# Column units beside layer 0's attention, logits ahead of the last value unit, and constant products in TensorE's waits

## What is computed

```python
ada = silu(c) @ w_ada[layer] + b_ada[layer]
sh_m, sc_m, g_m, sh_f, sc_f, g_f = split(ada, 6)
u = rmsnorm(h) * (1 + sc_m) + sh_m
proj = u @ w_in                       # q, k, v of 16 heads of 64
q, k = rmsnorm(q) * q_gain, rmsnorm(k) * k_gain
logits = q @ k.T * scale + cum_q - cum_k      # causal; cum: running sum of log forget gates
h = h + g_m * (softmax(logits) @ v) @ w_o
scores = sigmoid(u @ w_router); top 8 by scores + bias
h = h + g_f * (sum of weighted SwiGLU experts + shared expert)
```

## Time and profile before

| | us |
|---|---|
| median of 3 runs | 1393.61 |
| lowest, highest | 1393.27, 1396.72 |
| profiled execution, device time | 1396.53 |
| profiled execution, span of the core | 1394.8 |
| TensorE busy | 1338.6 (96%) |
| VectorE busy | 428.8 (31%) |
| ScalarE busy | 268.4 (19%) |

### The profile page before, as it was taken

One profiled execution on the slowest core, in us unless ns is written; L12 is line 12 of the kernel. 1 busy time (PEld: TensorE's weight loads), 2 busy tenths in 40 slices (PEclk: granted clock), 3 DMA queues, 4 the chain that ended last, 5 costly groups with the idle time before them and its releaser, 6 DMA issues.

```text
span 1394.8 us, 20069 instructions
## 1 busy us (share of the span) xinstructions
PE 1338.6 (96%) x8011; PEld 783.8 (56%) x8011; DVE 428.8 (31%) x969; ACT 268.4 (19%) x534; POOL 32.1 (2%) x82
## 2 busy tenths in 40 slices
PE   5998989999999999999899899899999999999997
PEld 1887865465444444444388788754564444444442
DVE  1799672101111111111183698611111111111111
ACT  2222531110111111011133563410110111111100
POOL 4000000001000000000000000000010000000000
PEclk9999999999999999999999999999999999999999
DMA  9999666999999999999999602579999999999996
GB/s 381 390 421 421 266 247 260 385 421 361 423 420 421 422 421 421 421 421 421 421 417 420 252 1 90 220 307 383 420 362 422 420 421 422 421 421 422 420 421 286
DMA packets 71774, 512.94 MB, mean 368 GB/s; under 512 B 8240, under 2 KB 8448, under 8 KB 9728
## 3 DMA queue, kind: packets, MB, share of 16 engines
q1 hardware_dynamic: 70560, 509.64, 88.6%
q0 software_dynamic: 832, 1.39, 0.5%
q10 hardware_dynamic: 288, 0.61, 0.1%
HBM read 510.55 MB, written 1.05 MB: 367 GB/s over the span
## 4 chain that ended last, share of the span: by engine, by line
PE 80%; DMA 8%; DVE 7%; ACT 2%; issue 2%; SPq 1%; DVEq 0%; ACTq 0%
PE PS L987 24%; PE PS L977 13%; PE PS L995 12%; PE PS L1011 11%; PE PS L565 6%; DMA ring<-in_w_in_a_units 4%; DMA ring<-in_w_exp 4%; DVE ring L614 2%; PE PS L737 2%; PE PS L1023 2%; SPq L1397 1%; PE PS L692 1%; PE PS L1852 1%; PE PS L1032 1%; PE PS L716 1%
## 5 line engine op out<-in xcount | busy, mean ns | idle before, releaser
L987 PE MATMUL PS<-ring,scratch 128*32 128x512 f32 (+2 forms) x2176 | 353.7, 593 | 6.7 <-DMA ring<-in_w_exp 5.3
L987 PEld LDWEIGHTS PS<-ring,scratch 128*32 128x32 f32 (+2 forms) x2176 | 111.0, 122 | 242.3 <-issue 240.6
L1342 DVE TENSOR_TENSOR scratch<-PS,gate_row 128x512 f32<-128x512 f32 x100 | 69.2, 692 | 462.3 <-PE PS L995 462.3
L977 PEld LDWEIGHTS PS<-scratch,u 128*128 128x128 f32 x1600 | 186.2, 194 | 38.4 <-issue 36.5
L977 PE MATMUL PS<-scratch,u 128*128 128x128 f32 x1600 | 195.4, 281 | 1.4 <-ACT scratch L1206 1.4
L995 PE MATMUL PS<-ring,scratch 128*32 128x512 f32 (+2 forms) x1088 | 182.2, 596 | 3.4 <-DMA ring<-in_w_exp 2.2
L1011 PE MATMUL PS<-scratch 128*128 128x512 f32 x384 | 172.7, 592 | 0.0
L565 PE MATMUL PS<-ring,uT 128*128 128x256 f32 x672 | 148.6, 380 | 3.6 <-DMA ring<-in_w_in_a_units 3.4
L1214 ACT ACTIVATE scratch<-PS 128x256 f32<-128x256 f32 x50 | 19.2, 384 | 672.9 <-PE PS L987 672.9
L565 PEld LDWEIGHTS PS<-ring,uT 128*128 128x128 f32 x672 | 126.3, 190 | 22.6 <-issue 4.2
L1330 DVE TENSOR_TENSOR scratch<-scratch,PS 128x256 f32<-128x256 f32 x50 | 21.1, 422 | 329.7 <-ACT scratch L1214 329.7
(11 more groups left out here) (346 smaller groups left out, 856.9 us busy)
## 6 DMA issues: line engine op xcount, KB each, us to landing
ring<-in_w_exp SPq DMA_DIRECT2D x384, 1024.0 KB, 16.4
ring<-in_w_ada_columns SPq DMA_DIRECT2D x48, 1024.0 KB, 25.6
ring<-in_w_in_a_units SPq DMA_DIRECT2D x12, 1024.0 KB, 27.5
ring<-in_w_ada_units SPq DMA_DIRECT2D x8, 1024.0 KB, 16.1
ring<-in_w_cmp_units SPq DMA_DIRECT2D x8, 1024.0 KB, 24.0
ring<-in_w_sh_units SPq DMA_DIRECT2D x6, 1024.0 KB, 13.7
ring<-in_w_kv_b_units SPq DMA_DIRECT2D x6, 1024.0 KB, 22.4
ring<-in_w_o_a_units SPq DMA_DIRECT2D x4, 1024.0 KB, 26.4
```

The source lines that it names most:

```text
L977: mm = pe_.matmul(PS[:, bank, i * w:(i + 1) * w], u[:, t, k * P:(k + 1) * P], hot[:, t, :], start=(t == 0), stop=(t == NT - 1))
L987: mm = pe_.matmul(PS[places, GU, :], x[:, kk, places], gate_and_up, start=(kk == 0), stop=(kk == KC - 1))
L1342: dve.tensor_tensor(y_rows[:, half * 512:(half + 1) * 512], PS[:, Y0 + half, :], gate_row[:, half * 512:(half + 1) * 512], ALU.mult).then_ ...
```

## The change

The diff does five things. Column units: the first 12 qkv units carry 16 in place of 24, and the other 8 come behind the last qkv unit and are processed one per attention batch (`columns_of_fox`, as `beside`). Logits: those of batch 0 are computed ahead of the last value unit; for that the value units go to banks 2, 6, 7, 6, and ScalarE loads the exponential's table ahead of the last copy of values. Products of a constant: in layer 0's attention ahead of `weigh` (8, 3, 6, 3, 3, 3 for batches 0 to 5, 124 columns each), two of 512 columns between the two tiles of normed rows (at three places), ten of 512 columns ahead of the wait for the mask in each layer's routing, and three of 512 ahead of the gates in layer 1's attention. The stage's `dve_vectors` moves behind attention, and a scaling of a gain moves behind the gate's diagonal.

```diff
-COLS_OF_QKV = [2, 2, 1, 2, 1, 2, 1, 2, 3, 3, 3, 2]
+COLS_OF_QKV = [2, 2, 1, 1, 1, 1, 1, 1, 1, 2, 2, 1]
+COLS_BESIDE_FOX = 8
...
+    order += [("cols", next(early)) for _ in range(COLS_BESIDE_FOX)]
...
+        V_BANK = [2, 6, 7, 6]
...
-                if kind == "nsa" and b in BUSY_BEFORE_HEADS:
-                    pe_keep_busy(pe_, BUSY_BEFORE_HEADS[b], heads_bank(kind, b), slice(4 * (DH + 1), 512 - P))
+                if b in BUSY_BEFORE_HEADS[kind]:
+                    pe_keep_busy(pe_, BUSY_BEFORE_HEADS[kind][b], heads_bank(kind, b), slice(4 * (DH + 1), 512 - P))
...
-        BUSY_BEFORE_HEADS = {0: 1, 1: 1, 2: 1, 3: 1, 4: 4}
+        BUSY_BEFORE_HEADS = {"fox": {0: 8, 1: 3, 2: 6, 3: 3, 4: 3, 5: 3}, "nsa": {0: 1, 1: 1, 2: 1, 3: 1, 4: 4}}
...
             for t in range(NT):
+                if t and tag in BUSY_BEFORE_NORMED:
+                    pe_keep_busy(pe_, 2, BUSY_BEFORE_NORMED[tag][1])
                 pe_.wait_ge(rows_normed, NT * NORMED.index(tag) + t + 1)
...
+            pe_keep_busy(pe_, 10, Y0 + 1)
             pe_.wait_ge(routing["mask_ready"], layer + 1)
...
             for j in range(12):
-                if j == 11:
-                    pe_.wait_ge(sem("fox_v"), 1)
-                elif j >= 3:
+                if j == 9:
+                    pe_.wait_ge(forget_rows, 5)
+                elif j == 11:
+                    pe_.wait_ge(sem("fox_copied"), 8)
+                    pe_.wait_ge(sem("fox_normed"), 8)
+                    pe_logits(pe_, "fox", fox_batches, fox_keys, 0)
+                    pe_.wait_ge(sem("fox_v"), 2)
+                elif 3 <= j <= 8:
                     pe_.wait_ge(sem("fox_normed"), j - 2)
-                pe_rows_unit(pe_, AT["qkv", j], j % 3, uT)
+                pe_rows_unit(pe_, AT["qkv", j], V_BANK[j - 8] if j >= 8 else j % 3, uT)
...
-            pe_.wait_ge(forget_rows, 5)
-            pe_.wait_ge(sem("fox_copied"), 8)
+            pe_logits(pe_, "fox", fox_batches, fox_keys, 1)
             pe_.wait_ge(sem("fox_v"), 4)
...
-            for b in range(2):
-                pe_logits(pe_, "fox", fox_batches, fox_keys, b)
...
                     pe_.wait_ge(sem("cmp_raw_copied"), 1)
+                    pe_keep_busy(pe_, 3, 4)
                     pe_.wait_ge(sem("gates_ready"), 1)
...
-            act_table(act, ACT.Exp)
+                elif j == 2:
+                    act_table(act, ACT.Exp)
...
-            dve.wait_ge(params, 16 * N_PARAMS)
-            done(dve.tensor_scalar(gain_qb[:, :], gain_qb[:, :], QK_SCALE, None, ALU.mult))
-            dve_vectors(done, 1, [(OF_LAYER[0] + SC_F, 1), (OF_KV + 1, 2)])
+            def columns_of_fox(b):
+                dve_columns(dve, [next(early) for _ in range(COLS_BESIDE_FOX // len(fox_batches))])
...
-            dve_attention(done, "fox", fox_batches, fox_finish)
+            dve_attention(done, "fox", fox_batches, fox_finish, columns_of_fox)
+            dve_vectors(done, 1, [(OF_LAYER[0] + SC_F, 1), (OF_KV + 1, 2)])
...
             dve_gate_diag(done, 0)
+            dve.wait_ge(params, 16 * N_PARAMS)
+            done(dve.tensor_scalar(gain_qb[:, :], gain_qb[:, :], QK_SCALE, None, ALU.mult))
```

More of the change, by code:

```diff
@@ L1621, in turn_unit, with fox_keys @@
                 mm.then_inc(sem("fox_turned"), 1)
+            def fox_keys(br, pair):
+                return kT_a[:, pair, :]
             for j in range(12):
-                if j == 11:
-                    pe_.wait_ge(sem("fox_v"), 1)
-                elif j >= 3:
+                if j == 9:
[6 more added lines that the diff above has]
+                elif 3 <= j <= 8:
                     pe_.wait_ge(sem("fox_normed"), j - 2)
-                pe_rows_unit(pe_, AT["qkv", j], j % 3, uT)
+                pe_rows_unit(pe_, AT["qkv", j], V_BANK[j - 8] if j >= 8 else j % 3, uT)
                 if 1 <= j <= 8:
@@ L1636, in _ @@
                     forget_turn_rows()
-            pe_.wait_ge(forget_rows, 5)
-            pe_.wait_ge(sem("fox_copied"), 8)
+            pe_logits(pe_, "fox", fox_batches, fox_keys, 1)
             pe_.wait_ge(sem("fox_v"), 4)
-            def fox_keys(br, pair):
-                return kT_a[:, pair, :]
-            for b in range(2):
-                pe_logits(pe_, "fox", fox_batches, fox_keys, b)
             pe_attention(pe_, "fox", fox_batches, fox_keys,
@@ L1908, in _ @@
                 done(act.activation(v_a[:, :, 4 * j:4 * j + 4, 0:DH],
-                                    PS[:, (8 + j) % 3, :].rearrange("p (t h d) -> p t h d", t=NT, h=4), ACT.Copy),
+                                    PS[:, V_BANK[j], :].rearrange("p (t h d) -> p t h d", t=NT, h=4), ACT.Copy),
                      sem("fox_v"))
```

## The result

The changed kernel takes 1418.2 us (median of four, 1416.45 to 1418.88) against 1393.44 for the kernel before (four, 1392.41 to 1396.72): a ratio of 1.0172, interval 1.0159 to 1.0185. The sign was forecast; the time lies outside the range of 1400 to 1416, 9.7 us above the forecast. The profiled execution took 1418.54 with a span of 1416.8, 22.0 more than the span before.

What follows compares the result with a forecast made beforehand. The prediction took the path up to each layer's first expert product as the bound, since transfers restart with it. Terms 8.0 + 2.3 + 2.3 + 1.1 + 1.2 + 0.1 = 15.0 us, on the median 1393.61, gave 1408.5 us, range 1400 to 1416.

Steps and rivals of the forecast that it cites:

- the clock term of the attention: End of layer 0's attention: TensorE's clock falls; half of each bound taken, +2.1 before the row turns, -0.9 in them.
- the start: Start of layer 0's attention: mask 1 done at 128.0 instead of 131.9, a gain of 3.9 us.
- the forecast of 8.0: Layer 0's attention and row turns: 6.8 + 2.1 - 0.9 = +8.0 us, bounds 5.0 and 11.1.
- the ten products: Before each layer's routing mask: ranks 5.5 us later, 3.2 returned by the clock, net +2.3 per layer.
- who paces the attention: Layer 0's attention: VectorE becomes the bound, its eight column units taking 18.7 us against 9.7 us of waits.
- the narrow products at 0: Layer 0's attention: 26 products cost nothing in TensorE's waits for VectorE; 5.4 us if that cover were gone.
- ffn0 at 0.1, mix1 at 1.12, ffn1 at 1.36: Two products between row tiles at three places: forecast 0 at ffn0, +1.1 at mix1, +1.2 at ffn1.
- the three products before layer 1's compressed logits: Ahead of the gates in layer 1's attention: 2.6 us in a wait of 2.38, +0.1, bounds -0.5 and +1.3.
- delays ahead of a phase are paid in full: Ahead of either expert phase: a microsecond lost or won moves the transfer stream and the end by a microsecond.
- The offset: Whole kernel: the 15.0 us sum laid on the median 1393.61, not the profiled 1396.53, giving 1408.6 instead of 1411.5.
- the clock gives nothing back: Rival for attention and ten-product blocks: attention 11.1, both blocks at 5.5, 24.5 in all, 1418 us; chance 0.07.
- The other two: Rivals: attention stays paced by TensorE, 1396.7, chance 0.06; expert phases swallow the delays, 1393.6, chance 0.06.

Runs made afterwards that it cites:

- after_again: The changed kernel run once more with no edit; 1418.89 us, ratio 1.0184 to the kernel before.
- no_fox: The changed kernel without the 26 narrow products in layer 0's attention; 1418.66 us, ratio 1.0148 to the kernel before.
- ten_alone: The kernel before with only the ten products ahead of the routing mask wait added, in both layers; 1403.31 us, ratio 1.0053.
- three_of_ten: The kernel before with three products, not ten, added ahead of the routing mask wait in both layers; 1389.56 us, ratio 0.9962.
- order_only: The changed kernel with the columns put back ahead of the attention and no added products of a constant; 1392.74 us, ratio 0.9993.
- no_beside: The changed kernel with the columns put back ahead of the attention, all products kept; 1408.94 us, ratio 1.0077.
- tail_products: The changed kernel with more narrow products (5, 5, 8, 2) at batches 4 to 7 of layer 0's attention; 1412.65 us, ratio 1.0098.
- tail_again: The same kernel as tail_products, run once more on another chip; 1412.21 us, ratio 1.0142 to the kernel before.

## Why the prediction was wrong, step by step

**What failed: the clock term of the attention.** The mechanism was seen, its size was not: half of each bound was taken, +2.1 up to the row turns and -0.9 in them, +1.2 in all. Counted from the last value unit, the clock cost 3.1 up to the row turns (52.19 against 49.08 at full clock), and from there to the gate row 0.81 was lost where 0.9 should have come back. That is 2.7 of the 3.8 us that the attention and its row turns cost more than forecast (11.84 in place of 8.0). The other 1.1 is the start: mask 1 ended at 129.0 where 128.0 was forecast, mask 7 at 159.65 where it was 158.6, so the full-clock part is 7.9 in place of 6.8. What VectorE does between the two masks was sized rightly.

The clock's fall comes early or late, and the forecast of 8.0 fits the early one: with it the gate row stood 7.1 (after_again, whose last value unit also began 1.2 earlier) and 7.7 (no_fox) later than before. But the late fall is the commoner, as far as traces and times tell: three traces of five have it, and of the changed kernel's eight executions only one was as quick as 1412.97, the others took 1416.5 to 1422.0. The prediction went by the 8.36 busy of 10 with a fall behind it. This row decides less than it seemed to: ten_alone and three_of_ten have 8.26 and 8.23 in the same stretch and 1.00 behind it. After the change that stretch had 6.69, with one wait of 2.90 behind it.

**Mis-sized: the ten products.** 2.3 were forecast per layer, 3.07 and 3.12 measured, and 3.0 to 3.1 when removed or added alone. The ranks came 5.9 later, not 5.5: the block takes 8.69 us, not 8.53, and starts 1.06 behind the gate row, not 0.86. The clock gave 2.8 back, not 3.2. The Trainium skill's page "TensorE: Matmul & The Clock Gate", section "Back-to-back issue gap", has 216 ns for a product of 512 columns, by which the block would take an estimated 2.2 us; at 0.87 us each in the trace, that price does not hold for these fp32 products.

**Right:** who paces the attention (VectorE without a gap) and how long it takes between its masks; the narrow products at 0 (1418.89 with and 1418.70 without, on one chip) and that they cost their length without that cover (5.0 us measured in order_only against no_beside, 5.4 worked out); ffn0 at 0.1, mix1 at 1.12, ffn1 at 1.36; the three products before layer 1's compressed logits at 0.18; that delays ahead of a phase are paid in full. That no narrow product has a price beside VectorE's waits is also seen in the late falls above, 52.19 with them and 52.72 without.

**Not seen:** 0.62 and 0.34 at the ends of the two expert phases. In layer 0's, 32 products behind a 2.77 us wait for a transfer took 5.34 us, in part at half clock, where the same 32 took 3.64 before, behind a wait of 2.67.

**The offset.** The sum was laid on the median because the profiled execution of before was 2.9 above it. The profiled execution of the changed kernel is not above its median (1418.54 and 1418.2), so 2.8 of the 9.7 missed are this step. "The stages differ little between runs" was not so: the length of an execution goes with its mean granted clock, and where a single profiled execution lies among the others is no property that can be carried to the next kernel.

**The rivals.** The one of "the clock gives nothing back" gave 1418 and has the time right, by luck for the most part. The attention came to its upper bound, 11.03 against 11.1, but as 7.9 + 3.1 and not as 6.8 + 4.3, and each block did give 2.8 back, against its 0. The rest of its number is made up by the 0.8, the phase ends and the offset. The other two fell: the attention was paced by VectorE, and the transfers restarted only with the late L992.

## What to carry to other kernels

Work moved beside a stage must fit, piece by piece, into the waits of the engine that does it: two columns of 2.3 us at the places where VectorE waited 1.8 and 2.6 us were free, eight spread evenly made the attention 8.3 us longer at full clock. A product of a constant that holds TensorE's clock is worth its place only up to the length of the wait it fills, so count it with the measured duration: three won 2.7 us a layer, ten lost 3. Where a clock fall can come early or late, the sum has two values, not one between them: here some +8 and +12 up to the gate row. Give each a chance of its own, and let the range reach over both.

## What was not expected of the hardware

The same program's clock fell at another place in another execution: at about 160 us in one trace of the changed kernel and at about 155 in the next, and its executions took from 1412.97 to 1421.99 us on one chip, with mean granted clocks from 0.996 to 0.989. In the trace of tail_products it fell in layer 1's attention too (0.50 in 860 to 870, above); in that of tail_again, the same kernel, it stood at 1.00 there, and the span is 7.0 shorter (1409.3 against 1416.3). So the time of a single execution of this kernel is no measure of a change of a few us. The start of one operation isn't either: that of the last value unit differed by 1.4 us between executions of kernels that are alike up to there. The length of a stretch, from the start of one operation to that of another, is the better measure: from the last value unit to the row turns it was 40.80 or 40.81 in four of the five traces with the attention of before (41.25 in ten_alone), and 49.08 and 49.07 in the two of tail_products. What decides the place within an execution stays open.
